# A layer's operand buffers on 512-byte lines of a partition

## The reference, cut to what matters

```python
f = swiglu(rmsnorm(h, g_ffn1_pre), w_ffn1_gate, w_ffn1_up, w_ffn1_down)   # 2048 -> 5632 -> 2048
h = h + 0.5 * rmsnorm(f, g_ffn1_post)
z = rmsnorm(h, g_mix_pre) @ w_qkv + b_qkv
o = concat([rmsnorm(dilated_attention(...), g_out_a), rmsnorm(sink_swa_gqa(...), g_out_b)])
h = h + rmsnorm(o @ w_o + b_o, g_mix_post)
f = swiglu(rmsnorm(h, g_ffn2_pre), w_ffn2_gate, w_ffn2_up, w_ffn2_down)
h = h + 0.5 * rmsnorm(f, g_ffn2_post)
gate = sigmoid(rmsnorm(h, g_ple_pre) @ w_ple_gate)
h = h + rmsnorm(gate * (p @ w_ple_proj), g_ple_post)
```

## Time and profile before

| | |
|---|---|
| median of 3 runs | 1968.12 us (1967.27 to 1969.93) |
| span of the profiled execution | 1966.2 us |
| TensorE busy | 1952.7 us (99%), 8937 instructions |
| VectorE busy | 1044.1 us (53%) |
| ScalarE busy | 872.1 us (44%) |
| weight loads on TensorE | 1606.7 us (82%) |
| granted TensorE clock, mean | 0.999 |

### The profile page before, as it was taken

One profiled execution on the slowest core, in us unless ns is written; L12 is line 12 of the kernel. 1 busy time (PEld: TensorE's weight loads), 2 busy tenths in 40 slices (PEclk: granted clock), 3 DMA queues, 4 the chain that ended last, 5 costly groups with the idle time before them and its releaser, 6 DMA issues.

```text
span 1966.2 us, 24898 instructions
## 1 busy us (share of the span) xinstructions
PE 1952.7 (99%) x8937; PEld 1606.7 (82%) x8937; DVE 1044.1 (53%) x1202; ACT 872.1 (44%) x1115; POOL 13.5 (1%) x28
## 2 busy tenths in 40 slices
PE   9999999999999999999999999999999999999998
PEld 7888888888888888888888888888888888888886
DVE  5455454454444447565676654444454454444575
ACT  6444444444333335544454454444444443334463
POOL 0000000000000000000000000000000000000000
PEclk9999999999999999999999999999999999999999
DMA  7666666666555554644454466666666655555554
GB/s 246 189 188 191 192 183 191 190 185 196 188 192 193 192 191 155 191 140 140 132 174 166 139 204 189 184 192 192 187 188 191 192 187 196 190 191 196 190 192 140
DMA packets 187394, 361.04 MB, mean 184 GB/s; under 512 B 11376, under 2 KB 15808, under 8 KB 186816
## 3 DMA queue, kind: packets, MB, share of 16 engines
q1 hardware_dynamic: 186320, 356.69, 58.7%
q10 hardware_dynamic: 1008, 3.46, 0.5%
HBM read 358.01 MB, written 2.10 MB: 183 GB/s over the span
## 4 chain that ended last, share of the span: by engine, by line
PE 98%; DVE 1%; ACT 1%; issue 0%; POOL 0%; DVEq 0%; ACTq 0%; POOLq 0%
PE bank L417 31%; PE bank L419 31%; PE bank L418 31%; PE bank L446 2%; PE bank L616 1%; PE bank L624 1%; PE bank L638 0%; PE bank L639 0%; PE bank L617 0%; PE bank L483 0%; DVE w_rest L1015 0%; PE bank L637 0%; ACT w_high L750 0%; PE bank L590 0%; ACT x_high L775 0%
## 5 line engine op out<-in xcount | busy, mean ns | idle before, releaser
L1015 DVE TENSOR_TENSOR w_rest<-raw,w_high 128x1024 fp32r<-128x1024 f32 (+1 forms) x668 | 812.4, 1218 | 771.3 <-ACT w_high L750 769.2
L750 ACT CAST w_high<-raw 128x1024 fp32r<-128x1024 f32 (+1 forms) x668 | 695.8, 1043 | 917.7 <-PE bank L419 910.5
L417 PE MATMUL bank<-w_high,x_high 128*128 128x512 f32 (+1 forms) x1952 | 768.7, 394 | 1.7 <-DVE w_rest L1015 0.8
L419 PE MATMUL bank<-w_high,x_rest 128*128 128x512 f32 (+1 forms) x1952 | 757.7, 388 | 0.0
L418 PE MATMUL bank<-w_rest,x_high 128*128 128x512 f32 (+1 forms) x1952 | 756.4, 388 | 0.0
L417 PEld LDWEIGHTS bank<-w_high,x_high 128*128 128x128 f32 x1952 | 366.6, 188 | 81.0 <-issue 5.3
L419 PEld LDWEIGHTS bank<-w_high,x_rest 128*128 128x128 f32 x1952 | 366.5, 188 | 76.8
L418 PEld LDWEIGHTS bank<-w_rest,x_high 128*128 128x128 f32 x1952 | 367.0, 188 | 71.3
L417 PE MATMUL bank<-w_high,h_high 128*128 128x512 f32 x704 | 278.7, 396 | 0.0
L419 PE MATMUL bank<-w_high,h_rest 128*128 128x512 f32 x704 | 278.4, 395 | 0.0
L418 PE MATMUL bank<-w_rest,h_high 128*128 128x512 f32 x704 | 278.4, 395 | 0.0
(11 more groups left out here) (123 smaller groups left out, 581.2 us busy)
## 6 DMA issues: line engine op xcount, KB each, us to landing
raw<-in_w_ffn_gate SPq DMA_DIRECT2D x176, 512.0 KB, 4.4
raw<-in_w_ffn_up SPq DMA_DIRECT2D x176, 512.0 KB, 3.7
raw<-in_w_ffn_down SPq DMA_DIRECT2D x176, 512.0 KB, 4.3
raw<-in_w_qkv SPq DMA_DIRECT2D x64, 512.0 KB, 3.7
raw<-in_w_o SPq DMA_DIRECT2D x32, 512.0 KB, 3.7
raw<-in_w_ple_gate SPq DMA_DIRECT2D x32, 512.0 KB, 4.1
bias_row<-in_b_qkv SPq DMA_DIRECT2D x1, 2176.0 KB, 8.8
resid<-in_x SPq DMA_DIRECT2D x8, 256.0 KB, 6.9
```

Of the source, the lines that this page charges most:

```text
L417: nc.tensor.matmul(o[:, 0:width], xh, w_high[:, k, c, 0:width], start=first and c == 0, stop=False)
L419: ins = nc.tensor.matmul(o[:, 0:width], xr, w_high[:, k, c, 0:width], start=False, stop=last and c == CPS - 1)
L750: nc.scalar.copy(w_high[:, k, :, 0:width], raw[:, k, :, 0:width]).then_inc(w_high_done, 1)
L1015: nc.vector.tensor_tensor(w_rest[:, k, :, 0:width], raw[:, k, :, 0:width], w_high[:, k, :, 0:width].bitcast(F32), ALU.subtract).then_inc(w ...
```

## The change

The list starts at the next multiple of 32, which is again 16512. `gain_T` (320 bytes) and `sinks` (64) come first, so that `raw` starts at 16896 = 33 x 512. `sb` gets an argument: a buffer with `line=LINE` starts at a multiple of 512. It is given for raw, w_high, w_rest, x_high, x_rest, h_high, h_rest, p_high and p_rest. The shared area starts at a multiple of 512 too. `junk` has one half instead of two (1024 bytes less), and each square waits for the one before it. No other instruction is changed. By the sizes, w, x, resid, branch, gain_row and ident move from 128 to 0 bytes behind a multiple of 512, and the shared area, with h, p and z, from 160 to 0.

```diff
-        where = [(nc.sbuf_base + 127) // 128 * 128]
-
-        def sb(name, shape, dt=F32):
+        where = [(nc.sbuf_base + 31) // 32 * 32]
+        LINE = 512
+
+        def sb(name, shape, dt=F32, line=32):
             size = 4 if dt != BF16 else 2
             for d in shape[1:]:
                 size *= d
+            where[0] = (where[0] + line - 1) // line * line
             t = nc.alloc_sbuf_tensor_at(name, shape, dt, offset=where[0])
             where[0] += (size + 31) // 32 * 32
             return t
...
-        raw = sb("raw", [P, RING, CPS, NB])
-        w_high = sb("w_high", [P, RING, CPS, NB], F32R)
-        w_rest = sb("w_rest", [P, RING, CPS, NB], F32R)
-        x_high = sb("x_high", [P, KC, S], F32R)
-        x_rest = sb("x_rest", [P, KC, S], F32R)
+        NG = 5
+        gain_T = sb("gain_T", [P, NG * KC])
+        sinks = sb("sinks", [P, BH])
+        raw = sb("raw", [P, RING, CPS, NB], line=LINE)
+        w_high = sb("w_high", [P, RING, CPS, NB], F32R, line=LINE)
+        w_rest = sb("w_rest", [P, RING, CPS, NB], F32R, line=LINE)
+        x_high = sb("x_high", [P, KC, S], F32R, line=LINE)
+        x_rest = sb("x_rest", [P, KC, S], F32R, line=LINE)
...
-        gain_T = sb("gain_T", [P, NG * KC])
-        junk = sb("junk", [P, 2, NB], BF16)
+        junk = sb("junk", [P, NB], BF16)
...
+        where[0] = (where[0] + LINE - 1) // LINE * LINE
         turns_from = where[0]
-        h_high = sb("h_high", [P, FC, S], F32R)
-        h_rest = sb("h_rest", [P, FC, S], F32R)
+        h_high = sb("h_high", [P, FC, S], F32R, line=LINE)
+        h_rest = sb("h_rest", [P, FC, S], F32R, line=LINE)
...
-        p_high = sb("p_high", [P, PC, S], F32R)
-        p_rest = sb("p_rest", [P, PC, S], F32R)
+        p_high = sb("p_high", [P, PC, S], F32R, line=LINE)
+        p_rest = sb("p_rest", [P, PC, S], F32R, line=LINE)
...
-                if not (isinstance(q, int) and q < 2):
-                    act.wait_ge(squared, q - 1)
-                nc.scalar.activation(junk[:, t % 2, :], src, ACT.Square, accum_out=stat[:, job, t, b]
+                if not (isinstance(q, int) and q < 1):
+                    act.wait_ge(squared, q)
+                nc.scalar.activation(junk[:], src, ACT.Square, accum_out=stat[:, job, t, b]
                                      ).then_inc(squared, 1)
```

More of the change, by code:

```diff
@@ L184, in layer_program @@
         ident = sb("ident", [P, P])
-        NG = 5
         G_FFN1, G_MIX, G_O, G_FFN2, G_PLE = (KC * k for k in range(NG))
         gain_in = branch[0:(NG - 1) * KC, 0, T * NB:T * NB + P]
-        gain_T = sb("gain_T", [P, NG * KC])
-        junk = sb("junk", [P, 2, NB], BF16)
+        junk = sb("junk", [P, NB], BF16)
         stat = sb("stat", [P, NJOB, T, NBD])
@@ L195, in layer_program @@
         minus_half = sb("minus_half", [P, T])
-        sinks = sb("sinks", [P, BH])
         spare = sb("spare", [P, 4])
+        where[0] = (where[0] + LINE - 1) // LINE * LINE
         turns_from = where[0]
-        h_high = sb("h_high", [P, FC, S], F32R)
-        h_rest = sb("h_rest", [P, FC, S], F32R)
+        h_high = sb("h_high", [P, FC, S], F32R, line=LINE)
+        h_rest = sb("h_rest", [P, FC, S], F32R, line=LINE)
         turns_to = where[0]
```

## The result

The changed kernel takes 1954.70 us (median of 4 runs, 1954.43 to 1955.07), the kernel before 1967.76 us beside it: ratio 0.9931, interval 0.9919 to 0.9943. The forecast was 1954, the gain 14.3 us; measured are 13.1 between the medians and 13.6 between the spans.

A forecast was written before the change was run, and what follows sets the result against it. TensorE, busy 99% of the span, was taken as the bound: number of products times start distance. The median 1968.1 less 14.3 us for h and p, all else 0, gives 1953.8, say 1954; range 1860 to 1970, the forecast's own 1950 to 1960.

The forecast's parts named there:

- The main step: TensorE's 2160 h and p products go from 233.4 to x's 226.8 ns, 14.3 us gained; chance 0.42.
- x unchanged: TensorE's 5760 x products keep their relation to w and stay at 226.7 ns, giving 0.
- two far bounds: Fixed part of an x product, 13.3 ns now, could shrink to 2.1 or grow to the 20.0 of h.
- the nearest row: Today's pace of x products on w, 226.7 ns, taken to stay after the change.
- The lower end: Fixed part of x products at 2.1 ns, from transposes at 108.8 ns less 106.7 for 256 columns.
- Rival A: Operand starts off a line cause the fixed part; all products go to 215.5 ns, about 102 us gained, 1866 us; chance 0.28.
- Its count of 64-byte steps: Fixed parts 13.3 and 20.0 ns as 2 and 3 steps of 6.67 ns, matching offsets of 128 and 160 bytes.
- B: Nothing changes, h's 6.6 ns coming from something else: 1968 us, at most 1.5 more by the squares; chance 0.15.
- C: Slower: x products stop settling and go from 226.7 to 233.3 ns, 38 us, 2006 us without gain on h; chance 0.10.
- the reason given against it: Against C: x and w share the same place in a line before and after, today the faster pairing.
- the single scratch on the path: ScalarE squares come 0.10 to 0.37 us later, covered by waits for TensorE: 0, at most 1.5 us at 4 stage ends.
- The sum of waits for subtractions: Sign that squares show on the path: TensorE's waits for subtractions or gain products would exceed 0.8 us.

The follow-up runs named there:

- experiments 1 to 4: Kernel before, h, p, z at 128 bytes: 1953.46 us; kernel before, all buffers 32 bytes on: 1972.39; changed kernel, x 32 on: 1987.86; changed kernel, w 32 on: 2002.30.
- experiments 2 to 4: Kernel before with all buffers 32 bytes on: 1972.39 us; changed kernel with x 32 bytes on: 1987.86 us; changed kernel with w 32 bytes on: 2002.30 us.
- experiments 3 and 4: Changed kernel with x and what follows up to ident 32 bytes off a multiple of 512: 1987.86 us; with w instead: 2002.30 us.
- experiment 2: Kernel before with its whole list of buffers 32 bytes further on, stationary and moving operands keeping their relation: 1972.39 us.

## Why the prediction was right

**The main step held, with its reason.** The forecast took the distance of h on w from x's, since x and w lay at the same place in a line, and priced it at 2160 x 6.6 = 14.3 us. The steps measured 13.9 + 0.3 = 14.2, and experiments 1 to 4 show the cause by moving it about: what counts is the place of the stationary to the moving operand.

**x unchanged, from two far bounds.** Both ends (2.1 ns and 20.0 of fixed part) came near real prices, of other kernels: 2.5 ns with two-byte operands, 19.9 with 32 bytes between x and w. The choice of the nearest row was right. The lower end had no ground, though: it sets the 108.8 ns of a transpose against the 106.7 ns of 256 columns, and a transpose here is 128 columns wide. No row says why it should take the time of 256. That the two-byte products came out near it was luck.

**Rival A** (the start off a line is what costs 13.3 ns) is out: with all operands on a line x still steps at 226.7. Its count of 64-byte steps matched two points and nothing else; 64 bytes cost as much as 32. Its 215.5 ns exist, but two-byte operands buy them. **B** is out. **C** didn't come; experiments 2 to 4 bear out the reason given against it.

**One step failed: the single scratch on the path.** The text put it at 0, at most 1.5 us for the ends of stages, and it is at a start that it shows. The text named as queued behind a square the next gain product, the next cast and VectorE's sum. It left out the six DMA issues that stand there once, L863 and L864, and it looked at when ScalarE starts its instructions, not at how far its queue runs ahead. The loss is 1.7 us at that place and 1.2 by the end, half a microsecond coming back at the shared keys. The sum of waits for subtractions, the prediction's own sign for this, rose from 0.8 us to 2.2. The gain product, the cast and the sum did behave as told: from there to the end the delay of the single scratch against the kernel before changes by no more than 0.1 us from one instruction to the next, except at the shared keys, where it shrinks by 0.6. The measured median of 1954.70 is 0.9 us above the forecast sum of 1953.8, less than this term.

The weight-load rule of the Trainium skill ("TensorE: Matmul & The Clock Gate", Step-by-step: what each phase is for), that a load takes nothing from the running product, would have the distance between their operands cost nothing; experiments 3 and 4 disagree, where 32 bytes cost 6.0 to 6.6 ns a product. The 215.7 ns that the same section of the Trainium skill gives for 512 columns agree with the 215.8 measured with two-byte operands.

## What to carry to other kernels

When products of one shape step at different paces in different stages, look at where their operands lie before looking at anything else, and put stationary and moving operands of four-byte products at the same byte modulo 256 (measured as free are multiples of 512 and 256 itself); moving 32 bytes of tables would have done here. A wait added to an engine also stops its queue: list everything behind it that used to be issued ahead, above all DMAs, at each of its places. And see whether two-byte pieces are exact enough, which was worth six times the placement.

## What the runs showed of the hardware that I had not expected

- The cost of a distance between the operands isn't modulo 64 and doesn't grow or fall evenly: 32, 64 and 96 bytes cost about 6 to 7 ns a product, 128 some 5.7, 192 only 2, 224 again 6 to 7, 256 nothing.
- Four-byte operands at the best distance cost 226.7 ns for 512 columns and two-byte ones 215.8, both at granted clock 1.00.
- Misplaced loads aren't paid for one by one: with only every third x load off, and two thirds of the h loads off as well, x's mean step was 233.1 ns, as with all x loads off (233.2).
- A wait of TensorE of 3.57 us was followed by granted clock 0.50, with products 0.43 us apart, where one of 1.14 us at the same place was not (experiment 2).
